# A decoder trunk with top-2-of-8 experts: three of twelve weight loads an expert move from SyncE's queue to ScalarE's

## The reference, cut to what matters

```
def moe_swiglu(x, w_router, w_gu, w_down):
    logits = jnp.einsum('bsd,de->bse', x, w_router).astype(jnp.float32)
    top_val, top_idx = lax.top_k(logits, TOP_K)          # 2 of 8
    gates = jax.nn.softmax(top_val, axis=-1)
    ...
    for e in range(N_EXPERTS):
        out = out + gate_full[..., e:e + 1] * swiglu(x, w_gu[e], w_down[e])
```

## Time and profile before

| | |
|---|---|
| Median of 3 runs | 1371.88 us (1371.03 to 1373.02) |
| The profiled execution | 1374.07 us |
| Its span, first to last instruction | 1372.4 us |
| Expert stage, from the first to the last expert's products | 978.3 to 1290.4 us |
| PE, DVE, ACT busy over the span | 94%, 48%, 40% |

### The profile page before, as it was taken

How to read it: one execution, slowest core, us unless ns; L and a number is a source line. 1 busy time by engine, 2 the same in 40 slices (tenths; PEclk the granted TensorE clock), 3 DMA queues, 4 the chain that set the end, 5 groups by cost and what they waited for, 6 DMA issues and landing times.

```text
span 1372.4 us, 17426 instructions
## 1 busy us (share of the span) xinstructions
PE 1290.8 (94%) x6493; PEld 1087.2 (79%) x6494; DVE 654.7 (48%) x863; ACT 546.3 (40%) x744; POOL 46.4 (3%) x64
## 2 busy tenths in 40 slices
PE   7999999899999999998989999998789999999568
PEld 6889998588888878886876899985778798878457
DVE  5334444633333322325542554455655654567664
ACT  3225442632233222225332333335644644467722
POOL 0000000000000000000000000000100211011000
PEclk9999999999999999999999999999899999989879
DMA  7331123133333333212325642123875885589831
GB/s 186 93 107 47 47 62 92 31 104 96 101 97 92 113 106 105 84 53 81 87 77 79 80 72 55 54 78 99 279 262 157 293 273 178 178 288 311 317 137 62
DMA packets 197959, 175.45 MB, mean 128 GB/s; under 512 B 7248, under 2 KB 178320, under 8 KB 197904
## 3 DMA queue, kind: packets, MB, share of 16 engines
q1 hardware_dynamic: 194016, 160.53, 40.7%
q0 software_dynamic: 3312, 12.06, 2.3%
q10 hardware_dynamic: 576, 2.10, 0.4%
HBM read 164.71 MB, written 9.96 MB: 127 GB/s over the span
## 4 chain that ended last, share of the span: by engine, by line
PE 87%; DMA 4%; DVE 4%; ACT 3%; issue 2%; ACTq 0%; POOLq 0%; POOL 0%; DVEq 0%; SPq 0%
PE bank L694 27%; PE bank L695 26%; PE bank L696 26%; PE bank L791 2%; DVE w_lo L1632 1%; DMA x_back<-x_dram 1%; PE bank L1062 1%; DMA ring<-moe_w_down 1%; DMA y_dram<-y_tok,store_i 1%; DMA xg<-x_dram,gather_i 1%; DMA xg<-x_dram,token_i 1%; PE bank L1015 1%; PE bank L942 1%; PE bank L1110 0%; PE bank L881 0%
## 5 line engine op out<-in xcount | busy, mean ns | idle before, releaser
L1632 DVE TENSOR_TENSOR w_lo<-raw,w_hi 128x1024 fp32r<-128x1024 f32 (+4 forms) x208 | 287.1, 1385 | 210.8 <-ACT w_hi L1216 147.8
L694 PE MATMUL bank<-x_hi,w_hi 128*128 128x512 f32 x672 | 265.8, 396 | 15.3 <-DVE w_lo L1632 7.0
L695 PE MATMUL bank<-x_lo,w_hi 128*128 128x512 f32 x672 | 264.0, 393 | 0.0
L696 PE MATMUL bank<-x_hi,w_lo 128*128 128x512 f32 x672 | 263.6, 392 | 0.0
L1216 ACT CAST w_hi<-raw 128x1024 fp32r<-128x1024 f32 (+2 forms) x141 | 149.7, 1062 | 128.3 <-PE bank L696 128.3
L694 PE MATMUL bank<-w_hi,x_hi 128*128 128x256 f32 (+2 forms) x608 | 191.0, 314 | 8.7 <-DVE w_lo L1632 3.3
L695 PE MATMUL bank<-w_lo,x_hi 128*128 128x256 f32 (+2 forms) x608 | 188.1, 309 | 0.0
L696 PE MATMUL bank<-w_hi,x_lo 128*128 128x256 f32 (+2 forms) x608 | 187.9, 309 | 0.0
L694 PEld LDWEIGHTS bank<-x_hi,w_hi 128*128 128x128 f32 x672 | 127.6, 190 | 47.1 <-DVE w_lo L1632 14.0
L696 PEld LDWEIGHTS bank<-x_hi,w_lo 128*128 128x128 f32 x672 | 127.6, 190 | 27.1
L695 PEld LDWEIGHTS bank<-x_lo,w_hi 128*128 128x128 f32 x672 | 127.8, 190 | 25.7
(11 more groups left out here) (307 smaller groups left out, 1793.1 us busy)
## 6 DMA issues: line engine op xcount, KB each, us to landing
raw<-moe_w_gu SPq DMA_DIRECT2D x32, 768.0 KB, 6.3
raw<-ffn_w_gu SPq DMA_DIRECT2D x44, 512.0 KB, 3.8
raw<-a_w_qkv SPq DMA_DIRECT2D x24, 512.0 KB, 3.7
raw<-moe_w_down SPq DMA_DIRECT2D x16, 768.0 KB, 6.4
raw<-ffn_w_down SPq DMA_DIRECT2D x16, 704.0 KB, 4.3
ring<-moe_w_gu SPq DMA_DIRECT2D x16, 640.0 KB, 7.5
raw<-moe_w_gu SPq DMA_DIRECT2D x16, 640.0 KB, 5.1
raw<-ple_w_gate SPq DMA_DIRECT2D x16, 512.0 KB, 5.8
```

The lines of the kernel that those rows point to most:

```text
L694: pe.matmul(o, s_hi, m_hi, start=start, stop=False, skip_group_check=True)
L695: pe.matmul(o, s_hi, m_lo, start=False, stop=False, skip_group_check=True)
L696: return pe.matmul(o, s_lo, m_hi, start=False, stop=stop, skip_group_check=True)
L1632: return dve.tensor_tensor(dst, a, b, ALU.subtract)
```

## The change

Chunks 7, 9 and 11 of each expert are no longer issued by SP. ACT issues them in `until_turned`, right behind the casts of chunks 4, 6 and 8, after a wait for the low part of chunk 1, 3 or 5 (the slot's last user). Slots, sizes, sources and semaphores of the loads stay. SP issues the other nine in their old order with their old waits. The addresses hold the expert's number, a register, so ACT computes them as SP did.

```diff
@@ -92,6 +92,7 @@
 
 L0 = BASE["moe"]
 SLOTS = 6
+ACT_LOADS = (7, 9, 11)
 
 
 def slot_loads(e, c):
@@ -470,6 +471,23 @@
         CONSTS = 2
         block = ctx.enter_context(nc.Block())
 
+        def load_chunk(eng, e, c):
+
+            s = c % SLOTS
+            if c < 8:
+                half, up, kh = c // 4, c // 2 % 2, c % 2
+                col = up * FE + half * FC[0]
+                src = moe_w_gu[0][bass.ds(e, 1), kh * 4 * P:(kh + 1) * 4 * P, col:col + FC[half]]
+                eng.dma_start(flat(s, 4, FC[half]), src.rearrange("e (k p) n -> p (e k) n", p=P)).then_inc(raw_loaded[s], 16)
+                return
+            c -= 8
+            full, r0, col = (3, 2)[c // 2], c // 2 * 3 * P, c % 2 * 512
+            src = moe_w_down[0][bass.ds(e, 1), r0:r0 + full * P, col:col + 512]
+            eng.dma_start(flat(s, 3, 512)[:, 0:full, :], src.rearrange("e (k p) n -> p (e k) n", p=P)).then_inc(raw_loaded[s], 16)
+            if c >= 2:
+                src = moe_w_down[0][bass.ds(e, 1), (KE - 1) * P:FE, col:col + 512]
+                eng.dma_start(ring[s][0:FE_LAST, 1024:1536], src.rearrange("e p n -> (e p) n")).then_inc(last_loaded[c - 2], 16)
+
         @block.sync
         def _(sp_eng):
             def slot_free(q, j):
@@ -557,26 +575,10 @@
                 sp_eng.wait_ge(lo_ready, low_count(e, c))
 
             with experts(nc, sp_eng) as e:
-                for c in range(8):
-
-                    half, up, kh = c // 4, c // 2 % 2, c % 2
-                    col = up * FE + half * FC[0]
-                    src = moe_w_gu[0][bass.ds(e, 1), kh * 4 * P:(kh + 1) * 4 * P, col:col + FC[half]]
-                    raw_free(e, c)
-                    sp_eng.dma_start(flat(c % SLOTS, 4, FC[half]), src.rearrange("e (k p) n -> p (e k) n", p=P)
-                                     ).then_inc(raw_loaded[c % SLOTS], 16)
-                for c in range(4):
-
-                    full, r0, col = (3, 2)[c // 2], c // 2 * 3 * P, c % 2 * 512
-                    raw_free(e, 8 + c)
-                    src = moe_w_down[0][bass.ds(e, 1), r0:r0 + full * P, col:col + 512]
-                    s = (8 + c) % SLOTS
-                    sp_eng.dma_start(flat(s, 3, 512)[:, 0:full, :], src.rearrange("e (k p) n -> p (e k) n", p=P)
-                                     ).then_inc(raw_loaded[s], 16)
-                    if c >= 2:
-                        src = moe_w_down[0][bass.ds(e, 1), (KE - 1) * P:FE, col:col + 512]
-                        sp_eng.dma_start(ring[s][0:FE_LAST, 1024:1536], src.rearrange("e p n -> (e p) n")
-                                         ).then_inc(last_loaded[c - 2], 16)
+                for c in range(12):
+                    if c not in ACT_LOADS:
+                        raw_free(e, c)
+                        load_chunk(sp_eng, e, c)
 
             def load_gate(c):
                 if c < RAW:
@@ -1536,6 +1538,9 @@
                 def body(n):
                     for c in range(10):
                         deep_hi(e, c + DEEP - 1)
+                        if c + SLOTS in ACT_LOADS:
+                            act.wait_ge(lo_ready, low_count(e, c))
+                            load_chunk(act, e, c + SLOTS)
                         if c in (1, 5):
                             half = c // 4
                             act.wait_ge(chunk_done, 4 * q0 + 12 * e + c + 1)
```

## The result

The changed kernel took 1377.17 us (median of 20 runs, 1370.92 to 1381.73), the kernel before 1372.20 us (20 runs, 1367.48 to 1376.02). The ratio is 1.0037, with a 95% interval of 1.0026 to 1.0049: 5.0 us slower, where 2.9 were forecast and 1374.8 us named. The profiled execution took 1378.62 us with a span of 1376.9.

What follows compares the result with a forecast made beforehand. PE was taken to set the pace up to expert 7, where the transfers catch up. Terms 0 + 1.2 + 0 + 0 + 1.7 = 2.9 us on the median of 1371.88 gave 1374.8 us, range 1369.5 to 1381.5.

Steps and rivals of the forecast that it cites:

- Time of issue: ACT's issues 0.1 to 0.3 us behind the starts of the casts of chunks 4, 6 and 8.
- the rival in which ACT's DMA waits for its cast's end: Each moved load goes out 1.3 to 1.5 us later; 9.6 us, 1381.5 us; chance 0.14.
- Expert 3 unchanged: Two-tile expert 3 stays at 52.3 us, since landings of 10.1 us fit in a lead of 11.
- ACT's own time 0: 32 new DMA issues take ACT 11 to 14 us, beside running casts and in idle time; cost 0.
- Chunk 9, 1.2 us: Lands in 6.8 us against 6.4 of lead, delaying PE's product 0.4 us each in experts 0, 2 and 6.
- Chunk 7 at 0: One-tile experts: lands about on time, small lateness covered by ACT's idle time; cost 0, up to 0.5 us.
- Chunk 11 "late, and free": One-tile experts: up to 1.2 us late, free because DVE makes its low part after the product; cost 0.
- The tail, 1.7 us: Expert 7: later chunk 7 idles the DMA side 1.6 us, later chunk 11 delays x_back; bounds 0 and 3.3.
- 2.9 us of queueing: Part of x_back's 11.15 us load put down to queueing; delay of its issue is free up to that.
- gather rival: Expert 6's gather lands earlier, removing PE's 2.19 us wait and clock fall: 7.3 us back, 1367.5 us; chance 0.09.
- Fair sharing: Both queues share equally; chunk 11 of expert 7 lands in 6.0 us; about 1373 us; chance 0.08.

Runs made afterwards that it cites:

- run 3: Kernel before, all twelve loads from SyncE, plus four 2 KB DMAs an expert issued by ACT at the changed kernel's places; ratio 1.0010 against the kernel before.
- Run 9: Kernel before with chunk 7 alone issued by ACT, chunks 9 and 11 staying on SyncE; ratio 1.0042 against the kernel before.
- Run 8: Kernel before with chunk 11 alone issued by ACT, chunks 7 and 9 staying on SyncE; ratio 1.0050 against the kernel before.
- run 7: Changed kernel with SyncE's chunk 0 of the next expert also waiting for PE's chunk 4 of this one; ratio 1.0026 against the kernel before.
- run 10: Changed kernel with chunk 11 back on SyncE, chunks 7 and 9 still issued by ACT; ratio 1.0037 against the kernel before.
- run 5: Kernel before, unchanged, timed against itself and profiled once more; ratio 0.9993.
- run 11: Kernel before with ACT issuing chunk 7 behind the cast of chunk 3 and chunk 9 behind that of chunk 4, chunk 11 on SyncE; ratio 1.0006.

## Why the prediction was right, and where its sizes were off

- **Time of issue: right.** The issues lie 0.2 us behind the starts of the casts in expert 2, and chunk 7's in expert 7 lies 0.98 us ahead of its cast's start, so the rival in which ACT's DMA waits for its cast's end is refuted. The queue of 8 in strict order that the Trainium skill, "TensorE: Matmul & The Clock Gate", table of specifications, gives ScalarE agrees with that.
- **Expert 3 unchanged: right**, 52.30 and 52.30 us. The two-tile experts together took 0.4 us less.
- **ACT's own time 0: right within 0.2%**, run 3.
- **Chunk 9, 1.2 us: right mechanism, wrong size.** The landing was set at 6.8 us and came to 6.4, 7.0 and 7.8 in experts 0, 2 and 6. PE's waits grew from 0.35 us to 0.68, 1.22 and 2.00, together by 2.9 us in place of 1.2. In expert 5 the landing took 9.7 us, and the 3.98 us wait is more than the two waits (0.35 + 2.19) it took the place of: 1.4 us that were set at 0.
- **Chunk 7 at 0: not contradicted, but its landing was.** It was set at 6 to 6.8 us; in experts 6 and 7 it took 7.8 and 7.9 us, and the casts waited 2.7 and 2.8 us for it. Still, PE had no wait of 0.3 us or more there before the one for `he`, and the casts of chunk 9 behind waited for their own landings (0.66 and 0.96 us). Run 9 shows that chunk 7 moved alone does cost.
- **Chunk 11 "late, and free": the reason was incomplete.** I had looked at the order behind the product and not at `het_lo`, which stands behind chunk 11's low part. Run 8 and run 7 show PE waiting for it. In the changed kernel it doesn't come to that, and the ratio without chunk 11 (run 10) is the same 1.0037. What is left of it is the first product of expert 1, 4.30 us in place of 3.32 (3.63 in run 10), which was set at 0.
- **The tail, 1.7 us: open, and not by the path that was forecast.** PE's last product of expert 7 ends 9.5 us later (1299.9 against 1290.4), since chunk 9 of expert 7 holds it up too: its load (8.16 us from 1275.60) stands in the chain that ended last, and x_back's load no longer does. x_back lands 5.6 us later (1300.3 against 1294.7), just when ACT is done with expert 7. ACT starts on it 5.8 us later than before (1300.49 against 1294.72), so its old wait for x_back hid 3.7 of the 9.5 us. Once issued (1290.99) it takes 9.3 us instead of 11.15, so part of the 2.9 us of queueing was indeed free. From the start of expert 7 to the end the changed kernel took 108.1 us, the first profile of the kernel before 109.4 and that of run 5 106.5: 1.3 less or 1.6 more.
- **The clock was left out** of the sum. New falls in experts 6 and 7 (3.4 us each) and a longer one in expert 2 (6.8 against 3.4 us) cost up to half their length, 1.7 us each, in the profile, and the shorter one in expert 5 (6.8 against 10.2) gives 1.7 back. Over the whole span the granted clock is 0.971 in both profiles, and over all executions 0.974 on average with the change and 0.973 without, so a lower clock does not explain the loss.
- **The gather rival** half came: the wait for gathered rows disappeared, but the time went into the wait for `he` just before it. Run 5 also shows that the 7.3 us it would have paid were partly chance.
- **Fair sharing** gave neither its landing nor its time. Chunk 11 of expert 7 took 7.0 us, not 6.0, and the kernel 1377.17 us, not 1373. Whether the queues share is a mixed picture (below).

So the forecast had the right way and the right first cause, late landings of chunk 9 in front of PE's transposes. Its 2.9 us against 5.0 is one term too small (chunk 9), two small ones set at 0 (expert 5 and the start of expert 1) and a tail whose size the profiles don't settle. That the total came this close is partly luck, as the profiled stage of experts ended 9.5 us later.

## What to carry to other kernels

Moving a load to another engine's queue also moves it to another place in time: it goes out when that engine's program gets there, and an engine that follows PE, as ACT does here, gets there late. Count the lead in the shortest stage, against the landing time of a busy queue, and follow what stands behind each late piece on every engine, not behind the first one only. Where a load has to come from a compute engine, put its issue in front of the work it is free at, not behind the work that is convenient.

## What was not expected of the hardware

In run 9 a load on ACT's queue did not start while an earlier one of SyncE's was under way. The DMA queues in the run with chunk 7 alone, first 1077.2 to 1080.8 us, then 1080.9 to 1085.2 (packets, MB, share of 16 engines; q1 is SyncE's, q10 ACT's, q0 POOL's):

```profile
q1 hardware_dynamic: 384, 0.75, 71.9%
q0 software_dynamic: 58, 0.24, 16.0%
```

```profile
q1 hardware_dynamic: 398, 0.75, 50.4%
q10 hardware_dynamic: 528, 0.66, 41.2%
q0 software_dynamic: 75, 0.24, 13.8%
```

ACT's chunk 7 was issued at 1076.09, and q10 has no packet at all before 1080.8; then all its 0.66 MB pass in 4.3 us, beside SyncE's next load. Of these two loads, issued 0.7 us apart, one was served after the other. But it isn't so always. The changed kernel in expert 7, 1279.8 to 1281 us:

```profile
q1 hardware_dynamic: 122, 0.25, 53.4%
q10 hardware_dynamic: 118, 0.24, 51.6%
```

Here both queues have half, which is the sharing packet by packet that the Trainium skill, "DMA: Bandwidth & Descriptors", section on queues, rings and completion order, describes. It was not seen in run 9, nor from 1283 to 1284 us of the changed kernel, where q1 had 103.2% and q10 1.7% with chunk 11 outstanding on it. What decides between the two was not tested.

The second surprise is the clock: behind PE's waits of 2.19 and 2.15 us at the same place of the same program, the granted clock was 0.50 for 10.2 us in one profile and 1.00 in the other. In run 11, behind 2.16 us, it was 0.50 for 10.0 us.
